# Experts that add into the output rows themselves, in a mixer layer with a routed expert stage

## The reference

```python
x = x + jnp.concatenate([yc, ya], axis=-1) @ w_out[l]
x = x + hierarchical_moe(rms_norm(x, norm_ffn_w[l]), ...)

def hierarchical_moe(xn, w_group, b_group, w_expert, b_expert, w1, w3, w2):
    ...
    gate = (p_g * jax.nn.softmax(top_v, axis=-1)).reshape(-1)       # one per (token, choice) pair
    ...
    def expert_block(args):
        xb, e = args
        h = jax.nn.silu(xb @ w1[e]) * (xb @ w3[e])
        return h @ w2[e]
    y = lax.map(expert_block, (xin, blk_e)).reshape(P, D)
    out = jnp.zeros((N + 1, D), jnp.float32).at[buf_tok].add(y * buf_gate[:, None])[:N]
```

## Time and profile before

| | |
|---|---|
| median of 3 runs | 1360.22 us (1358.24 to 1361.03) |
| the profiled execution's own time | 1359.96 us |
| span of that profile | 1358.3 us |
| PE, DVE, ACT, POOL busy | 1207.4, 870.9, 732.0, 147.1 us |
| expert loop, from the first gather issued to the last scatter issued | 718.2 to 1307.9 us |
| HBM read and written | 252.88 MB, 25.17 MB |

### The profile page before, as it was taken

The page is one execution under the profiler, slowest core; times in us unless marked ns, Lnnn a source line. Parts: engine busy times, 40 slices in busy tenths (PEclk is TensorE's granted clock), DMA queues, the critical chain, the costliest instruction groups (busy, mean ns, idle before and its releaser), DMA issues. The chain is left out here.

```text
span 1358.3 us, 16775 instructions
## 1 busy us (share of the span) xinstructions
PE 1207.4 (89%) x5870; PEld 977.8 (72%) x5870; DVE 870.9 (64%) x910; ACT 732.0 (54%) x918; POOL 147.1 (11%) x194
## 2 busy tenths in 40 slices
PE   5999989979988997699945999999999999999930
PEld 4887767757767776488834888888888888888830
DVE  4414444434426454543264999999999999999926
ACT  4322433543453243521104788888888888888820
POOL 1000000000010003010002011111111111111000
PEclk9999979989999998799957999999999999999975
DMA  6111100100000103331064899999999999999509
GB/s 199 39 31 32 32 16 16 32 15 16 16 16 16 32 16 124 147 148 47 31 263 154 322 379 384 382 384 387 380 384 384 381 383 385 389 381 378 204 17 371
DMA packets 57339, 261.89 MB, mean 193 GB/s; under 512 B 13008, under 2 KB 33488, under 8 KB 43984
## 3 DMA queue, kind: packets, MB, share of 16 engines
q1 hardware_dynamic: 46928, 240.31, 46.3%
q0 software_dynamic: 9216, 16.80, 3.3%
q10 hardware_dynamic: 1152, 4.19, 0.8%
HBM read 252.88 MB, written 25.17 MB: 205 GB/s over the span
## 5 line engine op out<-in xcount | busy, mean ns | idle before, releaser
L1245 DVE TENSOR_TENSOR e_lo<-W,e_hi 128x1024 fp32r<-128x1024 f32 x384 | 452.7, 1221 | 25.0 <-ACT e_hi L1239 21.9
L1239 ACT ACTIVATE e_hi<-W 128x1024 fp32r<-128x1024 f32 x384 | 403.3, 1060 | 96.3 <-PE ps L1210 96.3
L730 DVE TENSOR_TENSOR_SCAN kept<-kept 128x128 f32<-128x128 f32 (+7 forms) x64 | 90.3, 1410 | 222.9 <-ACT kept L587 190.1
L1208 PE MATMUL ps<-e_hi,xT_hi 128*128 128x512 f32 x512 | 204.3, 399 | 7.1 <-DVE e_lo L1245 7.1
L1210 PE MATMUL ps<-e_lo,xT_hi 128*128 128x512 f32 x512 | 201.6, 394 | 0.0
L1209 PE MATMUL ps<-e_hi,xT_lo 128*128 128x512 f32 x512 | 200.9, 392 | 0.0
L586 ACT ACTIVATE soft<-ps,q_scale 128x128 f32<-128x128 f32 (+7 forms) x54 | 38.0, 704 | 194.2 <-PE ps L456 183.0
L407 PE MATMUL ps<-xnT_hi,w_hi 128*128 128x512 f32 x320 | 129.2, 404 | 12.6 <-DVE u L698 6.0
L407 PE MATMUL ps<-xnT_lo,w_hi 128*128 128x512 f32 x320 | 129.2, 404 | 0.0
L407 PE MATMUL ps<-xnT_hi,w_lo 128*128 128x512 f32 x320 | 129.2, 404 | 0.0
L1208 PEld LDWEIGHTS ps<-e_hi,xT_hi 128*128 128x128 f32 x512 | 97.6, 191 | 26.8 <-issue 4.0
(11 more groups left out here) (211 smaller groups left out, 1801.2 us busy)
## 6 DMA issues: line engine op xcount, KB each, us to landing
W<-in_w_dram SPq DMA_DIRECT2D x96, 2048.0 KB, 10.1
w_raw<-in_w_in_dram SPq DMA_DIRECT2D x20, 512.0 KB, 4.0
yy<-y_rows SPq DMA_DIRECT2D x8, 1024.0 KB, 13.5
xt<-in_x_dram SPq DMA_DIRECT2D x8, 512.0 KB, 3.5
w_out_raw<-in_w_out_dram SPq DMA_DIRECT2D x4, 1024.0 KB, 8.4
xn_rows<-xn SPq DMA_DIRECT2D x8, 512.0 KB, 2.6
out_dram<-x ACTq DMA_DIRECT2D x8, 512.0 KB, 8.9
x<-in_x_dram SPq DMA_DIRECT2D x1, 3072.0 KB, 13.5
```

The lines of the kernel that those rows point to most:

```text
L730: dve.tensor_tensor_scan(back, back, back, 1.0, ALU.mult, ALU.min).then_inc(multiplied, 1)
L1208: pe.matmul(o, xs_hi[:, k], e_hi[:, p, cols], start=(k == 0), stop=False)
L1239: act.activation(e_hi[:, p], flat[:, p * D:(p + 1) * D], ACT.Copy).then_inc(s["hi_made"], 1)
L1245: dve.tensor_tensor(e_lo[:, p], flat[:, p * D:(p + 1) * D], e_hi[:, p], ALU.subtract).then_inc(s["lo_made"], 1)
```

## The change

- `x2` (the residual after the mixer) is stored to the output while the second norm runs, one store of 512 KB for each 128 tokens, on SP before that of `xn2`. The block's end waits for the stores.
- The gates are stored in HBM (`gate_rows`), each as a number of its own: two transfers of 1024 numbers on SP, behind four weight loads. The routing block's end waits for them.
- In the loop, POOL now issues four indirect transfers for an expert: the gather of tokens as before, the scatter of `acc` into the rows of the output (`pool_rows_out`), a gather of one gate for each slot (`pool_rows_in`), and a gather of the output's rows into `acc` (`pool_rows_start`). Since two experts may have a token in common, the row gather of expert e waits until the scatter of expert e-1 has landed.
- DVE makes the gated sum in `acc` out of PSUM (`dve_add`), between the splits for gate and up of round e+2; the copy `act_y` on ACT is gone. The copy of the turned hidden tile to `hidT_hi` goes from DVE to ACT (`act_hidT`).
- The overflow test goes in three steps of five blocks each. The lists get an extra column that points at no row.
- The last pass is gone.

POOL, in the counted loop over the experts: one expert's piece, before and now (`xg` holds gathered tokens, `xn_rows` is `xn2_rows`, `out_dram` the output; ISA and REGISTER rows compute semaphore values).

The diff, cut to its core:

```diff
                 for m in range(NT):
+                    sp.wait_ge(x2_made, 2 * m + 2)
+                    sp.dma_start(outv[m], x2[:, m]).then_inc(x2_stored, 16)
                     sp.wait_ge(xn2_made, m + 1)
                     sp.dma_start(xn2_rows_v[m], xn2[m % 2]).then_inc(xn2_stored[m % 2], 16)
+                sp.wait_ge(x2_stored, 16 * NT)
...
+                with nc.allow_non_contiguous_dma(reason="one number of each pair"):
+                    sp.wait_ge(gates_made, 1)
+                    for k in range(2):
+                        sp.dma_start(gate_view[k], gate[k]).then_inc(gates_stored, 16)
+                sp.wait_ge(gates_stored, 32)
...
-                link(dve.tensor_copy(over_list, ps[0:1, 3, 0:OVER + 1]))
+                link(dve.tensor_scalar(over_fill, ps[0:1, 3, 0:OVER + 1], 0.0, float(COLS), ALU.is_equal, ALU.mult))
+                link(dve.tensor_tensor(over_list, ps[0:1, 3, 0:OVER + 1], over_fill, ALU.add))
...
-            pe.wait_ge(s["y_made"], n)
+            pe.wait_ge(s["added"], n)
...
-        def act_y(act, s, n, b, rounds, down_start):
-            act.wait_ge(s["freed"], used(down_start + PIECES))
-            act.wait_ge(s["scattered"][b], 16 * rounds)
-            act.activation(y[b], psf[:, 5 * BANK:7 * BANK], ACT.Copy).then_inc(s["y_made"], 1)
+        def act_hidT(act, s, n):
+            act.wait_ge(s["hid_turned"], n + 1)
+            act.activation(hidT_hi.rearrange("p k t -> p (k t)"), ps[:, 4], ACT.Copy).then_inc(s["hidT_hi_made"], 1)
+
+        def dve_add(dve, s, n, b, rounds, down_start):
+
+            dve.wait_ge(s["freed"], used(down_start + PIECES))
+            dve.wait_ge(s["gates_in"][b], 16 * rounds)
+            dve.wait_ge(s["rows_in"][b], 16 * rounds)
+            dve.scalar_tensor_tensor(acc[b], psf[:, 5 * BANK:7 * BANK], slot_gate[b], acc[b], ALU.mult, ALU.add).then_inc(s["added"], 1)
...
-            dve.wait_ge(s["hid_turned"], n + 1)
-            dve.tensor_copy(hidT_hi.rearrange("p k t -> p (k t)"), ps[:, 4]).then_inc(s["hidT_hi_made"], 1)
...
-        def pool_scatter(pool, s, n, b, rounds, col, indexed):
+        def pool_rows_in(pool, s, n, b, rounds, col):
+
             if not (isinstance(rounds, int) and rounds == 0):
                 pool.wait_ge(s["scattered"][b], 16 * rounds)
-            pool.tensor_copy(idx_pair[b], slot_pair[:, bass.ds(col, 1)]).then_inc(s["indexed"], 1)
-            pool.wait_ge(s["indexed"], indexed)
-            pool.wait_ge(s["y_made"], n + 1)
+            pool.tensor_copy(idx_pair[b], slot_pair[:, bass.ds(col, 1)]).then_inc(s["out_indexed"], 1)
+            pool.tensor_copy(idx_out[b], slot_token[:, bass.ds(col, 1)]).then_inc(s["out_indexed"], 1)
+            pool.wait_ge(s["out_indexed"], 2 * n + 2)
             start_step(pool)
-            pool.indirect_dma_start(out=y_rows, out_offset=bass.IndirectOffsetOnAxis(ap=idx_pair[b].bitcast(U32), axis=0),
-                                    in_=y[b], in_offset=None,
-                                    bounds_check=PAIRS - 1, oob_is_err=False).then_inc(s["scattered"][b], 16)
+            pool.indirect_dma_start(out=slot_gate[b], out_offset=None, in_=gate_rows,
+                                    in_offset=bass.IndirectOffsetOnAxis(ap=idx_pair[b].bitcast(U32), axis=0),
+                                    bounds_check=PAIRS - 1, oob_is_err=False).then_inc(s["gates_in"][b], 16)
+
+        def pool_rows_start(pool, s, b):
+            start_step(pool)
+            pool.indirect_dma_start(out=acc[b], out_offset=None, in_=out_rows,
+                                    in_offset=bass.IndirectOffsetOnAxis(ap=idx_out[b].bitcast(U32), axis=0),
+                                    bounds_check=S - 1, oob_is_err=False).then_inc(s["rows_in"][b], 16)
+
+        def pool_rows_out(pool, s, n, b):
+            pool.wait_ge(s["added"], n + 1)
+            start_step(pool)
+            pool.indirect_dma_start(out=out_rows, out_offset=bass.IndirectOffsetOnAxis(ap=idx_out[b].bitcast(U32), axis=0),
+                                    in_=acc[b], in_offset=None,
+                                    bounds_check=S - 1, oob_is_err=False).then_inc(s["scattered"][b], 16)
 
...
+                def next_rows(e, b, rounds):
+
+                    pool_rows_out(pool, s_e, e - 1, 1 - b)
+                    pool_rows_in(pool, s_e, e, b, rounds, e)
+                    pool.wait_ge(s_e["scattered"][1 - b], 16 * (rounds + b))
+                    pool_rows_start(pool, s_e, b)
+
+                def gather_and_add(e, b, rounds):
                     pool_gather(pool, s_e, e + 2, b, e + 1, rounds + 1, e + 2)
-                    pool_gather_start(pool, s_e, b, 2 * e + 2)
-                    pool_scatter(pool, s_e, e - 1, 1 - b, rounds - 1 + b, e - 1, 2 * e + 3)
+                    pool_gather_start(pool, s_e, b, e + 3)
+                    next_rows(e, b, rounds)
...
-                with eng.Fori(0, OVER) as n:
-                    with eng.If(n < n_over):
-                        body(n)
+                with eng.Fori(0, OVER // OVER_STEP) as g:
+                    with eng.If(g * OVER_STEP < n_over):
+                        for i in range(OVER_STEP):
+                            body(g * OVER_STEP + i)
```

More of the change, by code:

```diff
@@ L1017, in hymba_moe_layer @@
         over_col = place("over_col", [P, 1])
-        slot_pair = keep("slot_pair", [P, COLS], I32)
-        slot_token = keep("slot_token", [P, COLS], I32)
+        slot_pair = keep("slot_pair", [P, COLS + 1], I32)
+        slot_token = keep("slot_token", [P, COLS + 1], I32)
         over_list = keep("over_list", [1, OVER + 1], I32)
         over_n = keep("over_n", [1, 1], I32)
+        over_fill = place("over_fill", [1, OVER + 1])
         iotas = sem("iotas")
@@ L1170, in hymba_moe_layer @@
         hidT_lo = place("hidT_lo", [P, FT, P], F32R)
-        y = [place(f"y{i}", [P, D]) for i in range(2)]
+        acc = [place(f"acc{i}", [P, D]) for i in range(2)]
         PIECES = KT * F // D
@@ L1177, in hymba_moe_layer @@
         idx_pair = [place(f"idx_pair{i}", [P, 1], I32) for i in range(2)]
+        idx_out = [place(f"idx_out{i}", [P, 1], I32) for i in range(2)]
+        slot_gate = [place(f"slot_gate{i}", [P, 1]) for i in range(2)]
         assert KT * F == FT * D
@@ L1181, in expert_sems @@
             return {n: sem(f"{tag}_{n}") for n in
-                    ("indexed", "turned", "xT_hi_made", "xT_made", "silu", "hidden", "hid_turned", "hidT_hi_made",
-                     "hidT_made", "y_made", "freed", "hi_made", "lo_made")} | {
+                    ("indexed", "out_indexed", "turned", "xT_hi_made", "xT_made", "silu", "hidden", "hid_turned", "hidT_hi_made",
+                     "hidT_made", "added", "freed", "hi_made", "lo_made")} | {
                 "gathered": [sem(f"{tag}_gathered{i}") for i in range(2)],
+                "rows_in": [sem(f"{tag}_rows_in{i}") for i in range(2)],
+                "gates_in": [sem(f"{tag}_gates_in{i}") for i in range(2)],
                 "scattered": [sem(f"{tag}_scattered{i}") for i in range(2)]}
@@ L1392, in _, with round_of @@
             def _(act):
-                def round_of(e, b, rounds, y_rounds=None, last=False):
+                def round_of(e, b, rounds, last=False):
                     act.wait_ge(expert_w[b][0], 16 * rounds)
                     act_split(act, s_e, gate_start(e), W1[b])
-                    if y_rounds is not None:
-                        act_y(act, s_e, e - 2, b, y_rounds, down_start(e - 2))
                     act.wait_ge(expert_w[b][1], 16 * rounds)
@@ L1513, in body @@
                     dve_split(dve, s_o, start + 2 * PIECES, W2[0])
+                    dve_add(dve, s_o, n, 0, n + 1, start + 2 * PIECES)
                 each_block(dve, body)
[L1517 to L1544 removed]
         return dict(locals())
```

96 lines of the change are left out of this document (47 added, 49 removed).

## The result

After: 1420.36 us in the median (1408.03 to 1430.61, 4 runs). Before, on the same chip: 1360.62. The ratio is 1.0405 (95% interval 1.0383 to 1.0428), so the change costs 4%; the execution of 1430.61 was a slow one, and the ratio leaves it out. The profiled execution took 1420.67 with a span of 1418.9, against 1358.3 before.

A forecast was written before the change was run, and what follows sets the result against it. The prediction took PE to bound the loop at 17.75 us a round. From 1360.0 it summed end -34.6, front +1, loop without wait +3, wait +63 and clock +11 to 1403.4, given as 1404, range 1328 to 1450.

The forecast's parts named there:

- What bounds the loop: Expert loop: PE bounds the 17.75 us round, DVE 0.76 behind; transfers look full, but three loads need only 14.8 us.
- rival A: Loop: the chain fits, L below 15.5 us, nothing waits; 1330, or 1348 if bytes cost +18; chance 0.30.
- The wait, +63: Loop: add waits for row gather, that for the previous scatter; mean period 20.1, 2.2 us over 17.85 in 28 intervals.
- L: Loop: time from a scatter's issue to the gathered rows' landing; taken as 20 us, period L + 2.3, no wait under 15.5.
- the row gather's last part falls free: Loop: loads cover the chain until about 20 us after the scatter, so the row gather ends without loads; L = 20.
- as nearly full: Loop: the gate gather's tiny pieces wait nearly like whole rows, landing 6.0 us behind the scatter, ahead of the row gather.
- The loop without the wait, +3: Loop: DVE loses a cast and gains the add, 17.6 us under PE's 17.75; 0.1 us in each of 29 rounds.
- The clock, +11: Loop: PE's clock is half behind a stall, 1.6 us lost, half hidden; 0.8 us, 14 times.
- The front, +1: Before the loop: gate transfers behind four loads land at 714 to 718 against DVE's 714.5; 0 to 4 us.
- The end, -34.6: After the last split: last pass gone -33.9, 12 fewer overflow tests -9.3, chain of scatter, row gather and add +8.6.
- Rival B: Loop: every interval is long, 22.3 us each for 1455 or 25.5 each for 1544; chance 0.10.
- C: Whole kernel comes out even: mean period 18.8 to 19.0 us, 1357 to 1363; chance 0.03.

The follow-up runs named there:

- the run with more rows: Kernel before plus one more gather a round (the spare gather) of the expert's rows into a buffer nobody reads, each waiting for the one before; 1387.34 us, ratio 1.0189.
- quarter loads: Changed kernel with loop loads of a quarter of the weights, all instructions, waits and indirect transfers kept; 1329.25 us, ratio 0.9767.
- without the row gather: The adding kernel with a plain scatter that overwrites rows in place of the adding one; no row gather or wait for its rows; 1328.08 us, ratio 0.9762.
- the adding kernel: Changed kernel whose scatter itself adds into the output rows, after the previous round's scatter landed; row gather and its wait gone; 1346.52 us, ratio 0.9899.
- experts by turns: Changed kernel with neighbouring rounds taking experts of different groups, so a row gather needs only the scatter of two rounds before; 1371.17 us (1374.19 with gathers issued later).

## Why the prediction came out right, and where it was off

The forecast was 1404 in 1328 to 1450, slower at 0.67. The time was 1420, in the forecast's own case: the mean interval of 20.9 lies in 19.0 to 21.9. But a part of the way there was wrong.

- **What bounds the loop.** "... and the transfers look full. They are not short on the mean" is the step that failed. The sum of 14.8 us for three loads in 17.75 left the indirect transfers out; the share of 0.98 was the true reading. In the first rounds of the run with more rows the loads' landings grow from round to round (10.2 to 12.8 us) while the rounds are still 17.75. The prediction had a price for this only in rival A, +18; the estimate from that run is 16.
- **The wait, +63.** Right in kind, and its place in the code as told: DVE idle ahead of the add (75.6 us), POOL ahead of the row gather, PE without pieces. Off in size: 12 long intervals of 24.1 where I had 14 of 22.3, 76.6 us over 17.75 in place of 62. L, taken as 20, was 21.8 on their mean, and it was made up of other parts: in the interval shown two loaded landings in a row, 12.1 and 11.4, not a slow gate gather and then a nearly free row gather. The step "the row gather's last part falls free" was wrong: until shortly before the rows were in, the engines ran at 422 GB/s. That L came near is in part luck. "Long and short by turns" held roughly, with one or two short ones behind each long one; the scatter behind a stall took 3.3 to 5.4, still less than the 6.0 supposed. How the 90 us divide between waits and bytes is not shown. Without the wait for the scatter 55 stay, with the chain taken out 42, and the bytes alone are an estimate of 16; with quarter loads or without the row gather it is 0. The chain needs the full queue to be long, so the two aren't separate causes.
- **The gate gather "as nearly full"** stood for 6 us of L. Left out of the changed kernel it gave nothing back, out of the adding one at most some 3 us in the whole loop. It is issued while POOL would wait for the scatter anyway. That tiny pieces wait as long as whole rows is borne out by neither run.
- **The loop without the wait, +3**: 0, by the quarter loads' 17.75.
- **The clock, +11**: 13.9 in the short intervals. With each of the twelve stalls (2.9 to 8.2 us of idle PE) the clock was half for 3.4 to 10.2 us. PE was busy for 52.9 us in these stretches, which is an estimate of 26 us lost at half speed. So about half was hidden, as supposed; what was too small was the loss for each stall, 2.2 us in place of 1.6.
- **The front, +1**: 0; the first gather goes out at 718.2 in both.
- **The end, -34.6**: -31.2. The chain behind the last split came as said (last scatter 12.8 us behind it in place of 4.4, 8.4 where I had 8.6). The tests gave 5.7 in place of 9.3, since PE's first one took 3.7 us.
- **Rival A** (the chain fits, 1330 to 1348) had two forms. The chain does fit with small loads, at 1329. With all transfers of this kernel kept and the chain out of the way it is 1371 and 1374, so the other form, 1348, was too low for the orders of transfers that were tried. By the Trainium skill's fit in "DMA: Bandwidth & Descriptors" (anatomy of one DMA on the gpsimd path) a scatter is an estimated 2.6 us. The runs show 3.2 to 3.3 with idle engines, 11.0 at a share of 0.98, 15.6 in the run with more rows: the fit has no term for a full queue.
- **Rival B** and **C**: no run of intervals was long throughout, and it didn't come out even.

The same page of the Trainium skill (rules for kernel authors) says that an accumulate reads its destination and writes it later, so that the earlier one's semaphore must be awaited; the adding kernel waits so. What the adding costs with full engines is what this case shows: 18.4 us. Of the slow branch, the Trainium skill's "Runtime: NRT & Kernel Launch" (instruction fetch mechanics) says that a taken branch to a target outside the fetched window forces a fetch by DMA before the engine goes on. The trace agrees as far as it shows: transfers of the instruction queues start inside the 3.7 us, at 1413.8 to 1414.3, and the length doesn't depend on whether three or five bodies are skipped.

**Open**: why the changed kernel without gate gathers was 0.5% slower; how the 55 us that stay without the wait for the scatter, and the 42 with experts by turns, divide into bytes, landings and POOL's order, since the same queue makes the first two; and whether a token gather issued ahead of POOL's waits gives some of them back. Whether a load order that leaves gaps for the chain would help wasn't tried.

## What to carry to other kernels

Before a transfer is added to a loop, read the share of the DMA engines in the loop's stretch, not the sum of its loads: at 0.98 there was no room for 4% more bytes, and with them every transfer took 4 to 6 us longer. A wait chain through DRAM (write, then read back) pays the landing time of the loaded queue twice, 21.8 us here on the mean of the long intervals against 8.6 idle; take its price from landings in the busiest stretch. Moving the last pass into the full loop saved 31 us at the end and cost 90 in the loop, while a transfer that adds at its target needs no rows gathered and won 1%. And look for a wait of its own in an experiment that is to price bytes alone: here the spare gather's wait for the one before was as long as the round.

## What the hardware showed that I had not expected

- When the scatters add, the queue of the indirect transfers takes 1.5 times the engines' time for the same bytes (5.2% against 3.4%, 70 against 45 us of all 16). Gathers are in both, so an adding scatter takes an estimated twice the time of a plain one, if half of the 45 are scatters. It lands in 6.2 us in place of 3.2 with idle engines, and shows no more bytes in the counters (HBM read 244.51 MB in both).
- The engines moved 422 GB/s in one stretch, where the loop's mean was 364 and a full round 382.
- PE's first taken branch over three or five unrolled bodies takes 3.4 to 3.7 us, the following ones 0.22; with one body it was 0.39 at most.
